# Attention heads of a two-layer backbone: weight loads on another queue, four landing buffers, the turn last in a slot

## The reference

```python
def attend_block(args):
    n, qn = args                       # one of 4 blocks of 128 queries
    kw = lax.dynamic_slice_in_dim(kp, n * BLOCK, BLOCK + 2 * WINDOW, axis=1)
    vw = lax.dynamic_slice_in_dim(vp, n * BLOCK, BLOCK + 2 * WINDOW, axis=1)
    s_win = jnp.einsum('bqkgd,bjkd->bkgqj', qn, kw).astype(jnp.float32) * scale
    s_ctx = jnp.einsum('bqkgd,bjkd->bkgqj', qn, k_ctx).astype(jnp.float32) * scale
    ...
    logits = jnp.concatenate([sink_logits(sink, s_win.shape[:-1]), s_ctx, s_win], axis=-1)
    p = jax.nn.softmax(logits, axis=-1)
    ...
    return (jnp.einsum('bkgqj,bjkd->bqkgd', p_ctx, v_ctx)
            + jnp.einsum('bkgqj,bjkd->bqkgd', p_win, vw))
```

## Time and profile before

| | us |
|---|---|
| median of three executions | 1415.17 (1410.56 to 1417.88) |
| the profiled execution | 1414.83, of which 1412.9 from first to last instruction |
| TensorE busy | 1372.3 (97%) |
| VectorE busy | 891.7 (63%) |
| ScalarE busy | 518.4 (37%) |
| GpSimd busy | 74.8 (5%) |
| the heads in this execution | from 383.21 (first scores) to 656.91 (last attend product) |

### The profile page before, as it was taken

How to read it: one execution, slowest core, us unless ns; L and a number is a source line. 1 busy time by engine, 2 the same in 40 slices (tenths; PEclk the granted TensorE clock), 3 DMA queues, 4 the chain that set the end, 5 groups by cost and what they waited for, 6 DMA issues and landing times.

```text
span 1412.9 us, 19130 instructions
## 1 busy us (share of the span) xinstructions
PE 1372.3 (97%) x7258; PEld 1141.3 (81%) x7258; DVE 891.7 (63%) x1407; ACT 518.4 (37%) x798; POOL 74.8 (5%) x145
## 2 busy tenths in 40 slices
PE   4999999999999999999999999999999999999998
PEld 2788888888878788787888888888888888887887
DVE  6545656556888888796645776677666334474434
ACT  5323422244565544454222432122353223323332
POOL 0001111011000000000101010001000000010000
PEclk9999999999999999999999999999999999999999
DMA  9996567656655656476766666356523333365333
GB/s 384 408 389 247 180 214 251 191 186 204 195 174 164 175 152 187 144 208 217 263 193 193 194 184 204 97 167 191 171 90 105 95 100 94 108 201 182 110 90 120
DMA packets 98881, 262.17 MB, mean 186 GB/s; under 512 B 10976, under 2 KB 36592, under 8 KB 97392
## 3 DMA queue, kind: packets, MB, share of 16 engines
q1 hardware_dynamic: 77184, 182.55, 39.8%
q0 software_dynamic: 19936, 73.38, 16.3%
q10 hardware_dynamic: 1680, 5.10, 1.0%
HBM read 242.64 MB, written 18.36 MB: 185 GB/s over the span
## 4 chain that ended last, share of the span: by engine, by line
PE 77%; DMA 10%; DVE 5%; SPq 4%; issue 2%; ACT 1%; DVEq 0%; ACTq 0%
PE ps L1546 76%; DMA blocks<-cond_row 7%; SPq L424 4%; DMA kvmem<-in_ctxT 1%; DVE w_lo L948 1%; DMA raw<-in_mod 1%; DMA modchunk<-blocks 1%; DMA cond_row<-blocks 1%; DVE cond_row L1255 1%; DVE tmp L1074 1%; SPq L382 0%; DVE kvmem L1241 0%; DVE tmp L1241 0%; DVE kvmem L1136 0%; ACT tmp L720 0%
## 5 line engine op out<-in xcount | busy, mean ns | idle before, releaser
L1546 PE MATMUL ps<-h_hi,w_hi 128*128 128x512 f32 x1592 | 622.9, 391 | 2.5 <-DVE w_lo L948 1.5
L1546 PE MATMUL ps<-h_lo,w_hi 128*128 128x512 f32 x1592 | 619.6, 389 | 0.0
L1546 PE MATMUL ps<-h_hi,w_lo 128*128 128x512 f32 x1592 | 619.0, 389 | 0.0
L948 DVE TENSOR_TENSOR w_lo<-raw,w_hi 128x1024 fp32r<-128x1024 f32 x206 | 251.4, 1220 | 364.3 <-ACT w_hi L519 363.9
L519 ACT CAST w_hi<-raw 128x1024 fp32r<-128x1024 f32 x206 | 216.2, 1050 | 592.7 <-PE ps L1546 592.6
L1546 PEld LDWEIGHTS ps<-h_hi,w_hi 128*128 128x128 f32 x1592 | 299.2, 188 | 69.0 <-issue 4.9
L1546 PEld LDWEIGHTS ps<-h_hi,w_lo 128*128 128x128 f32 x1592 | 299.1, 188 | 62.3
L1546 PEld LDWEIGHTS ps<-h_lo,w_hi 128*128 128x128 f32 x1592 | 299.3, 188 | 58.3
L954 DVE CUSTOM_DVE_ANT_0 modchunk<-modchunk,cond_row 128x1024 f32<-128x1024 f32 x128 | 154.7, 1220 | 19.8 <-DMA modchunk<-in_modb 19.4
L465 POOL DMA_DIRECT2D modchunk<-in_modb x128 | 67.6, 528 | 828.0 <-DVE modacc L954 812.4
L1546 PE MATMUL ps<-k_hi,q_hi 128*128 128x256 f32 (+1 forms) x96 | 30.4, 317 | 6.0 <-DVE stat L1241 3.7
(11 more groups left out here) (233 smaller groups left out, 1394.4 us busy)
## 6 DMA issues: line engine op xcount, KB each, us to landing
raw<-in_weights SPq DMA_DIRECT2D x208, 512.0 KB, 3.6
modchunk<-in_modb POOLq DMA_DIRECT2D x128, 512.0 KB, 4.6
raw<-in_mod SPq DMA_DIRECT2D x32, 512.0 KB, 9.3
modchunk<-in_mod SPq DMA_DIRECT2D x16, 512.0 KB, 7.4
cond_row<-in_mod SPq DMA_DIRECT2D x16, 512.0 KB, 9.0
blocks<-cond_row SPq DMA_DIRECT2D x24, 320.0 KB, 2.9
blocks<-cond_row SPq DMA_DIRECT2D x24, 256.0 KB, 2.3
main<-in_xT SPq DMA_DIRECT2D x4, 1024.0 KB, 8.4
```

Of the source, the lines that this page charges most:

```text
L948: nc.vector.tensor_tensor(low, src, high.bitcast(F32), ALU.subtract).then_inc(lo_ready, 1)
L1546: return nc.tensor.matmul(out, lhsT, rhs, start=start, stop=stop, skip_group_check=True)
```

## The change

Three edits, all within the heads; the fourth point tells what stays:

1. SyncE issues only stores and fetches of turned blocks. The 32 weight units that fell in the heads are issued by GpSimd, behind its early modulation rows, each as soon as its `raw` buffer is free; they signal semaphores of their own (`unit_landed`). The last of them stands behind GpSimd's wait for the last `turned_lo`.
2. Four landing buffers in place of two: three lie in the modulation's chunk buffer. A fetch of step g waits for `turned_lo` of step g - 4.
3. On VectorE `turn_blocks` comes last in a slot: behind the two value pieces in slot 1, and behind `lo` in slots 2, 4, 6, 8 and 10.
4. In SyncE's queue the order of stores and fetches stays as it was: store k, fetch k, store k + 1. The order on ScalarE and TensorE is unchanged.

```diff
+TURN_SLOTS = 4
+HEAD_UNITS = (G_Z * HALVES + 6, G_O * HALVES + 6)
...
-        blocks_in = [cond_row[:, 2 * most:3 * most], chunk_flat[:, 0:most]]
+        blocks_in = [cond_row[:, 2 * most:3 * most]] + [chunk_flat[:, n * most:(n + 1) * most] for n in range(TURN_SLOTS - 1)]
...
             def fetch_blocks(i, k):
                 g, cols = i * STEPS + k, key_tiles(k) * P
-                run = cols // 4
+                run, slot = cols // 4, g % TURN_SLOTS
                 sp.wait_ge(written[g % 2], 16 * (g // 2 + 1))
-                if g >= 2:
-                    sp.wait_ge(pt_ready, g - 1)
+                if g >= TURN_SLOTS:
+                    sp.wait_ge(pt_ready, g + 1 - TURN_SLOTS)
...
             for i in range(KV_HEADS):
-                for k in range(SLOTS):
-                    if 1 <= k <= STEPS and (k > 1 or i == 0):
-                        fetch_blocks(i, k - 1)
-                    if k < STEPS and (k or i == 0):
-                        store_blocks(i, k)
-                    if k == NEXT_SCORES and i + 1 < KV_HEADS:
-                        store_blocks(i + 1, 0)
-                    if k == NEXT_SCORES + 1 and i + 1 < KV_HEADS:
-                        fetch_blocks(i + 1, 0)
-                    if k in UNIT_SLOTS:
-                        load_unit((G_Z + i) * HALVES + UNIT_SLOTS.index(k) + 6)
-                load_unit((G_Z + i) * HALVES + HALVES + 5)
+                for k in range(STEPS):
+                    store_blocks(i, k)
+                    fetch_blocks(i, k)
...
             load_chunks(1, M_O * HALVES // 2)
+
+            def load_unit(u):
+                pool.wait_ge(lo_ready, u + 1 - RAW_SLOTS)
+                pool.dma_start(raw[:, u % RAW_SLOTS].rearrange("p a n -> p (a n)"), weights[u]).then_inc(unit_landed[u % RAW_SLOTS], 16)
+
+            last_in_heads = HEAD_UNITS[1] - 1
+            for u in range(HEAD_UNITS[0], last_in_heads):
+                load_unit(u)
             pool.wait_ge(row_stored, 16)
             pool.wait_ge(pt_ready, KV_HEADS * STEPS)
             pool.dma_start(cond_row[:], row_scratch.broadcast_to([P, D])).then_inc(row_back, 16)
+            load_unit(last_in_heads)
...
             def turned_hi(i, k):
 
                 g = i * STEPS + k
-                act.wait_ge(pt_landed[g % 2], 64 * (g // 2 + 1))
+                act.wait_ge(pt_landed[g % TURN_SLOTS], 64 * (g // TURN_SLOTS + 1))
...
-                    if k < STEPS and (k or first):
-                        turn_blocks(i, k)
                     if k == 1:
                         piece(i * PIECES + 4, v_lo[:, 0:BLOCKS], values[:, :, i * P:(i + 1) * P], v_hi[:, 0:BLOCKS])
                         piece(i * PIECES + 5, v_lo[:, BLOCKS:], values_c[:, :, i * P:(i + 1) * P], v_hi[:, BLOCKS:])
                     if k in UNIT_SLOTS:
                         lo(i + G_Z, UNIT_SLOTS.index(k) + 2)
+                    if k < STEPS and (k or first):
+                        turn_blocks(i, k)
```

More of the change, by code:

```diff
@@ L140 @@
 TURN_LAG = 3
+TURN_SLOTS = 4
+HEAD_UNITS = (G_Z * HALVES + 6, G_O * HALVES + 6)
+assert (HEAD_UNITS[1] - HEAD_UNITS[0]) % RAW_SLOTS == 0
 NEXT_KEYS, NEXT_SCORES = 12, 14
@@ L311, in landed_tiles @@
         def landed_tiles(i, k):
-            return blocks_in[(i * STEPS + k) % 2][:, 0:key_tiles(k) * P].rearrange("p (a t c) -> p t a c", a=4, c=QUADRANT)
+            return blocks_in[(i * STEPS + k) % TURN_SLOTS][:, 0:key_tiles(k) * P].rearrange("p (a t c) -> p t a c", a=4, c=QUADRANT)
         S_END = 6 * 512 - 256
         raw_landed = [sem(f"raw_landed{i}") for i in range(RAW_SLOTS)]
+        unit_landed = [sem(f"unit_landed{i}") for i in range(RAW_SLOTS)]
         chunk_landed = [sem(f"chunk_landed{i}") for i in range(2)]
@@ L349, in build @@
         written = [sem(f"written{i}") for i in range(2)]
-        pt_landed = [sem(f"pt_landed{i}") for i in range(2)]
+        pt_landed = [sem(f"pt_landed{i}") for i in range(TURN_SLOTS)]
         row_stored, row_back = sem("row_stored"), sem("row_back")
@@ L418, in fetch_blocks @@
                 g, cols = i * STEPS + k, key_tiles(k) * P
-                run = cols // 4
+                run, slot = cols // 4, g % TURN_SLOTS
                 sp.wait_ge(written[g % 2], 16 * (g // 2 + 1))
-                if g >= 2:
-                    sp.wait_ge(pt_ready, g - 1)
+                if g >= TURN_SLOTS:
+                    sp.wait_ge(pt_ready, g + 1 - TURN_SLOTS)
                 for j in range(4):
-                    sp.dma_start(blocks_in[g % 2][j * QUADRANT:(j + 1) * QUADRANT, 0:cols].rearrange("c (a x) -> c a x", a=4),
+                    sp.dma_start(blocks_in[slot][j * QUADRANT:(j + 1) * QUADRANT, 0:cols].rearrange("c (a x) -> c a x", a=4),
                                  turn_scratch[g % 4, :, j * run:(j + 1) * run].rearrange("(a c) x -> c a x", a=4)
-                                 ).then_inc(pt_landed[g % 2], 16)
-            before_heads = G_Z * HALVES + 6
+                                 ).then_inc(pt_landed[slot], 16)
+            before_heads, after_heads = HEAD_UNITS
             load_units(1, (before_heads - HALVES) // RAW_SLOTS)
@@ L511, in hi @@
                 else:
-                    act.wait_ge(raw_landed[j % RAW_SLOTS], (n * 2 + (j // RAW_SLOTS - 1 + RAW_LANDINGS)) * 16)
+                    u = n * HALVES + j
+                    if HEAD_UNITS[0] <= u < HEAD_UNITS[1]:
+                        act.wait_ge(unit_landed[u % RAW_SLOTS], ((u - HEAD_UNITS[0]) // RAW_SLOTS + 1) * 16)
+                    else:
+                        missed = (HEAD_UNITS[1] - HEAD_UNITS[0]) // RAW_SLOTS if u >= HEAD_UNITS[1] else 0
+                        act.wait_ge(raw_landed[u % RAW_SLOTS], (u // RAW_SLOTS - 1 + RAW_LANDINGS - missed) * 16)
                     src = raw[:, j % RAW_SLOTS]
```

1 line of the change is left out of this document (removed).

## The result

| | median us of four executions | lowest to highest | ratio to before (95% interval) |
|---|---|---|---|
| before | 1416.39 | 1410.56 to 1417.88 | |
| changed | 1436.66 | 1435.86 to 1437.08 | 1.015 (1.012 to 1.018) |

The change made the kernel slower by 1.5%, some 20 us. I had forecast 1416.6 us, no change to speak of, with a range that ended at 1426 us.

A forecast was written before the change was run, and what follows sets the result against it. TensorE was taken as the bound, with some 17 us of waits and clock to win in the heads. Slot delays less the tails left +1.4 us; +1.3 us for a landing and -0.9 us for the clock gave +1.8: 1416.6 us, range 1409 to 1426.

The forecast's parts named there:

- Weights from GpSimd: Weight loads leaving SyncE's queue in the heads: price 0, since a landing of 4.6 us is covered by some 25 us.
- The chain of waits: Profile's waits by line: stores of turned blocks 7%, issue of fetches 4%; these 11%, some 155 us, cannot be the price.
- The turn behind the weights: VectorE, slots 2 to 10: the low part waits for ScalarE's cast; slot 6 grows 1.0 us, from 4.55 to 5.55 us.
- Slot 1: VectorE, slot 1 of a head: the value pieces fill the turn's wait for the exponential, 0.8 us less.
- The tails: Ends of heads: TensorE's waits there take in the delay, 0.72, 1.36, 3.56 and 2.74 us after heads 0 to 3.
- the first rival: Ends of heads don't take in the delay, as blocks land late: 9.8 us slower, 1424.6 us; chance 0.19.
- The clock: TensorE around its longest wait: 1.8 us of products lost at the low clock; a shorter wait wins back 0.9 us.
- The buffers: SyncE's landing buffers: two more take away its 24.3 us of buffer waits, which may merely move to the landing of stores.

The follow-up runs named there:

- f2: Kernel before with the 32 weight loads in the heads moved to GpSimd's queue; two landing buffers and VectorE's old order kept: 1431.95 us, ratio 1.0153.
- e1: Changed kernel with VectorE's order of before; weight loads on GpSimd's queue and four landing buffers stay: 1432.12 us, ratio 1.0113.
- g4: Changed kernel with the weight loads back on SyncE; four landing buffers and the new VectorE order stay: 1422.48 us, ratio 1.0052.
- g1: e1 with GpSimd's loads in slots 2, 4, 6, 8 and 10 waiting for a semaphore raised behind that slot's store: 1418.53 us, ratio 1.0029.
- g2: Kernel before, all on SyncE, with the loads of slots 2 to 10 moved behind that slot's fetch, ahead of the next store: 1449.83 us, ratio 1.0246.
- f3: e1 with the 32 weight loads issued by ScalarE, a hardware queue, in place of GpSimd: 1433.31 us, ratio 1.0168.
- e2: Kernel before with the new VectorE order alone; weights on SyncE, two landing buffers: 1421.45 us, ratio 1.0047.
- f1: Kernel before with four landing buffers and nothing else changed: 1409.29 us, ratio 0.9995.
- f4: e1 without the 32 weight loads in the heads; the buffers keep what they held: 1404.05 us, ratio 0.9954.

## Why the prediction was wrong

**The step that failed is "Weights from GpSimd".** It says "The price is 0", and bounds what the move does between nothing and a gain of 7.4 us. I had asked whether the loads would be late for their own user, and that cover is real: in none of these traces does ScalarE's cast wait for a weight load in the heads, and TensorE's wait for `w_lo` is 1.9 us in all in the changed kernel. I had not asked whom a load meets. In the kernel before, SyncE's order puts each load of slots 2 to 10 behind a store, and the load slips into the time in which the store's landing is awaited. Freed from that order it starts when `lo` is done, and in the changed kernel the turn and its store follow `lo`: the load of most slots is then 1.3 us or more ahead of the store, and ten stores in place of three take over 4.0 us. f2 puts the price of the move at 1.53% with two buffers, e1 at 1.13% with four, and in the changed kernel it is 14 of the 20 us (g4). g1 shows that the moment makes most of it, g2 that a second queue is not needed. (In e1, f2 and f3 TensorE does wait 5 to 7 us for `w_lo`. In its longest such wait, 5.66 us in f3, the cast stood in ScalarE's queue behind a cast of blocks that waited 7.95 us to land.) The sentence from the Trainium skill that spreading issues over engines saves issuing time only (DMA: Bandwidth & Descriptors, Issuing engines are not separate DMA queues) agrees with all this: f3's hardware queue did as badly as GpSimd's. I drew from it that nothing would change, which it does not say. The Trainium skill's rule on VectorE holding up GpSimd's issues (SBUF — State Buffer, SBUF: two separate sides) was not the cause: f3 does without GpSimd.

**The chain of waits had said so, and I set it aside.** "These are 11% ... and so cannot be the price" was right as a price of now. But 7% through `blocks<-cond_row` also says that a store's landing often has no slack, and so what a longer landing may cost: 2.4 us more on each of some ten stores is the size of the loss. My row for the landing wait, 76.7 us, had no lower or upper bound for a landing beside other traffic, though the earlier trace rows showed 8.75 us for a fetch beside a reload.

**The turn behind the weights** was right in mechanism and size: 5.60 us against 5.55 us forecast, waits of 2.21 and 1.69 us against about 2 and 1.6 us. With the order alone (e2) attend 2 of heads 0 and 1 waits 0.75 us each, against 0.8 us forecast. Slot 1 as well.

**The tails** were half right. With the order alone (e2) the last attend of head 2 waits no more and the small waits after heads 0 and 1 shrink, as forecast; the sum for this kernel should have been +1.8 us, and it is +6.6 us. In the last head two waits of 1.11 us remain where 2.74 us were to be won, so the term was over-sized, and the low clock is not avoided (0.91 over 400 to 420 us). In the changed kernel the opposite happened at the ends of heads 0 and 2, and the first rival (late blocks, "nothing is recovered") named the place: 1424.6 us by its sum. Its reason does not hold, though. It took the late landing to come from later turns, and in e2 and g4, where the turns are as late, head 2's last attend waits no more.

**The clock**: I took 0.9 us back, since the longest wait was to shrink. That one did, from 2.58 us to 1.06 us (at 662.51), but waits of 2.21 and 2.52 us stand elsewhere, and each was followed by a stretch at the lower level (last section): 1.7 us lost in place of 0.9 us won.

**The account of the whole.** To the end of the heads TensorE's waits grew by 30.7 - 13.7 = 17.0 us. They are 28 in place of 18, and 10 more at 0.16 us are 1.6 us; the clock adds 1.7 us. Together 20.3 us, against 21.2 us between the two spans (1434.1 and 1412.9 us). So what a wait costs was about right, and which waits there would be was wrong.

**The buffers** at nothing: right (f1, 0.9995).

**The chances**: 0.21 for slower was too little. No rival had the mechanism: loads that hold up the stores were not among them.

## What to carry to other kernels

When a transfer moves to another queue, ask not only whether it comes in time for its user, but what it will now start ahead of: the old queue's order may be what kept a bulk load out of the way of a small transfer whose landing everything waits for. If it must move, tie its start to the small transfer's issue by a semaphore; here that took back three quarters of the loss. And a chain of waits that runs through a landing warns of what a slower landing costs, even where little is to be won by a faster one: 20 stores slowed cost 2.5% (g2), and leaving all loads out of the heads won 0.5% (f4).

## What the runs showed of the hardware

- A store of 256 to 320 KB takes 2.3 us in the median to its fetch when no loads are about (f4). Behind a load of 512 KB issued 0.5 us ahead of it, it takes 4.40 to 5.15 us (g2, 20 stores, one queue). It is the same from GpSimd (e1: 4.95 us with the load 0.67 us ahead) and from ScalarE (f3: 5.11 us, 0.57 us ahead), and 29 of 33 stores still take over 4.0 us with the load 1.0 to 2.0 us ahead. A load issued some 0.8 us behind the store leaves it at 2.39 us (g1, median of 19).
- TensorE's clock: it granted 0.83 over the 10 us around the wait of 2.21 us and 0.91 over the 20 us around that of 2.52 us, and 1.00 around those of 1.82 us and 2.36 us (attend 0 of head 0, at 408.14). So the length of the one wait does not decide it. The first two are 3.4 and 3.6 us at the lower of its two levels (1.2 and 2.4 GHz), right behind the wait. That costs 3.5 us of products, against 1.8 us before. Windows of the changed kernel:

```profile
405.00:415.00 10.00, 7.64 (x41) 6.53 (x40) 7.66 (x15) 4.03 (x9) 0.38 (x1) 1.00 0.64 185
450.00:460.00 10.00, 8.03 (x40) 6.49 (x39) 7.09 (x14) 4.89 (x10) 0.00 (x0) 1.00 0.27 83
480.00:490.00 10.00, 7.79 (x35) 6.91 (x34) 6.90 (x14) 2.99 (x8) 0.00 (x0) 0.83 0.59 177
595.00:615.00 20.00, 17.48 (x82) 15.08 (x81) 14.91 (x28) 7.66 (x17) 1.06 (x2) 0.91 0.35 117
```
